# Gated recurrent mixer with its products grouped by array shape and its norm inside the loop; spatial gate with its bias added on VectorE

## The reference

```python
f = lb + (1.0 - lb) * sigmoid(fl);  k = 1.0 - f;  b = cumsum(log(f))      # within a chunk
q_dec, k_inv, k_state = q * exp(b), k * exp(-b), k * exp(b_last - b)
A = where(causal, q_dec @ k_inv.T, 0)                # 64 x 64 in each chunk
U = k_state.T @ iv                                   # 128 x 128 in each chunk
s_prev = scan(state = exp(b_last) * state + U)       # eight chunks, one after the other
o = A @ iv + q_dec @ s_prev
o = o * rsqrt(mean(o * o) + 1e-6) * onorm_g * silu(g);   return o @ w_out
```

```python
mixed = einsum('gts,bnsgc->bntgc', tril(sgu_w), v) + transpose(sgu_b)[:, :, None]
return (u * mixed) @ w_out
```

## Time and profile before

| | before |
|---|---|
| median of 3 runs (lowest to highest) | 4350.57 us (4349.04 to 4352.63) |
| the profiled execution, its own time | 4350.56 us |
| its span in the trace | 4348.7 us |
| TensorE matmuls, busy | 3777.4 us (87%) |
| VectorE, busy | 2104.5 us (48%) |
| ScalarE, busy | 1231.2 us (28%) |
| mean granted TensorE clock | 0.904 of full speed |

### The profile page before, as it was taken

The page is one execution under the profiler, slowest core; times in us unless marked ns, Lnnn a source line. Parts: engine busy times, 40 slices in busy tenths (PEclk is TensorE's granted clock), DMA queues, the critical chain, the costliest instruction groups (busy, mean ns, idle before and its releaser), DMA issues. The chain is left out here.

```text
span 4348.7 us, 57875 instructions
## 1 busy us (share of the span) xinstructions
PE 3777.4 (87%) x23603; PEld 3021.9 (69%) x23603; DVE 2104.5 (48%) x2957; ACT 1231.2 (28%) x1606; POOL 0.2 (0%) x4
## 2 busy tenths in 40 slices
PE   7899999988899988889989989979248757989998
PEld 6567887767788875568867668868147744667886
DVE  3475655343574553553443363442755546435434
ACT  2353333231342322232232132221411122223222
POOL 0000000000000000000000000000000000000000
PEclk9999999985899998889999799989569976999999
DMA  3101222210122221022222012221000010022221
GB/s 130 58 0 68 97 90 94 97 68 0 49 97 97 97 80 68 10 78 90 94 92 77 28 70 97 97 74 66 10 7 4 7 36 1 29 87 76 90 97 67
DMA packets 43411, 279.58 MB, mean 64 GB/s; under 512 B 5920, under 2 KB 6816, under 8 KB 10598
## 3 DMA queue, kind: packets, MB, share of 16 engines
q1 hardware_dynamic: 36576, 266.35, 17.3%
q10 hardware_dynamic: 6662, 10.69, 0.7%
HBM read 274.92 MB, written 2.11 MB: 64 GB/s over the span
## 5 line engine op out<-in xcount | busy, mean ns | idle before, releaser
L213 PE MATMUL PS<-XH,WH 128*128 128x512 f32 (+1 forms) x2704 | 1041.4, 385 | 27.3 <-DVEq L95 23.5
L214 PE MATMUL PS<-XL,WH 128*128 128x512 f32 (+1 forms) x2704 | 1042.7, 386 | 0.0
L215 PE MATMUL PS<-XH,WL 128*128 128x512 f32 (+1 forms) x2704 | 1037.6, 384 | 0.0
L146 DVE TENSOR_TENSOR WL<-W,WH 128x2048 fp32r<-128x2048 f32 x254 | 582.1, 2292 | 886.4 <-ACT WH L136 880.9
L136 ACT ACTIVATE WH<-W 128x2048 fp32r<-128x2048 f32 x254 | 485.6, 1912 | 1227.6 <-PE PS L303 682.3
L213 PEld LDWEIGHTS PS<-XH,WH 128*128 128x128 f32 x2704 | 510.0, 189 | 145.6 <-issue 20.2
L214 PEld LDWEIGHTS PS<-XL,WH 128*128 128x128 f32 x2704 | 509.2, 188 | 108.8 <-issue 2.2
L215 PEld LDWEIGHTS PS<-XH,WL 128*128 128x128 f32 x2704 | 510.4, 189 | 104.4
L301 PE MATMUL PS<-HH,WH 128*128 128x512 f32 (+1 forms) x1024 | 401.9, 392 | 10.5 <-DVEq L95 9.3
L302 PE MATMUL PS<-HL,WH 128*128 128x512 f32 (+1 forms) x1024 | 400.1, 391 | 0.0
L303 PE MATMUL PS<-HH,WL 128*128 128x512 f32 (+1 forms) x1024 | 399.9, 391 | 0.0
(11 more groups left out here) (435 smaller groups left out, 4217.4 us busy)
## 6 DMA issues: line engine op xcount, KB each, us to landing
W<-in_weights SPq DMA_DIRECT2D x254, 1024.0 KB, 4.8
X<-in_x ACTq DMA_DIRECT2D x1, 2048.0 KB
out<-X ACTq DMA_DIRECT2D x1, 2048.0 KB, 7.1
consts<-in_consts ACTq DMA_DIRECT2D x1, 1026.0 KB
bias<-bias_spread ACTq DMA_DIRECT2D x4, 256.0 KB
w_gd<-in_w_gd ACTq DMA_DIRECT2D x1, 640.0 KB
rope<-in_c_rope ACTq DMA_DIRECT2D x1, 528.0 KB
ws<-in_ws ACTq DMA_DIRECT2D x1, 512.0 KB
```

The costliest lines, as they stand in the source:

```text
L146: P.e.tensor_tensor(K.WL[:, s, :], K.W[:, s, :], K.WH[:, s, :].bitcast(F32), ALU.subtract).then_inc(P.sem("weights_split"), P.adds("weight ...
L213: P.e.matmul(out, wh[:, k, c], xh[:, k, r], start=(k == 0), stop=False)
L214: P.e.matmul(out, wh[:, k, c], xl[:, k, r], start=False, stop=False)
L215: last = P.e.matmul(out, wl[:, k, c], xh[:, k, r], start=False, stop=(k == KT - 1))
```

## The change

In the mixer:

- `h_i` is no longer staged; TensorE transposes `i1` directly. The loops are written out, eight steps each.
- TensorE runs the eight products with `aT` together, before it waits for the states, and then the eight with the state.
- `h_ks` is made by one multiplication of `h_ki` by exp(b) at the chunk's end. The subtraction and the third exponential go.
- The copy of `ksT` moves from VectorE to ScalarE.
- The norm moves into the loop: one product 512 columns wide with a matrix of 1/128 (`inv_dv`) gives the means on every partition; ScalarE takes (mean + eps)^(-1/2) as exp(-0.5 ln(...)) (`root`); VectorE multiplies two heads later (`normed`), and the split follows. A table set with both functions is loaded ahead. The diagonals, spreading products, reciprocal and square root after the loop go.

In the gate the bias is loaded as 128 equal rows (512 KB instead of 4 KB) and added by VectorE, which then multiplies by `u2`; the bias products go. The copy of `s_vT` moves from VectorE to ScalarE.

```diff
 # Hgrn, VectorE
-            P.e.tensor_tensor(K.h_ks[:, b, :], K.h_k[:, :], K.h_ks[:, b, :], ALU.mult)
+            P.e.tensor_tensor(K.h_ki[:, b, :], K.h_k[:, :], K.h_ki[:, b, :], ALU.mult).then_inc(P.sem("ki_ready"), P.adds("ki_ready"))
+            P.e.tensor_tensor(K.h_qd[:, b, :], K.q1h[:, t, :], K.h_eb[:, b, :], ALU.mult).then_inc(P.sem("qd_ready"), P.adds("qd_ready"))
+            P.e.wait_ge(P.sem("ki_ready"), P.due("ki_ready", 0))
+            P.e.tensor_tensor(ks, ki, ends, ALU.mult).then_inc(P.sem("keys_ready"), P.adds("keys_ready"))
...
+        def normed(t):
+            o = K.f1[:, t, :]
+            P.e.wait_ge(P.sem("o_root"), P.due("o_root"))
+            P.e.scalar_tensor_tensor(o, o, K.p["hgrn_onorm_g"][:, t:t + 1], K.o_sq[:, t % 2, :], ALU.mult, ALU.mult).then_inc(P.sem("o_normed"), P.adds("o_normed"))
+            P.e.wait_ge(P.sem("o_normed"), P.due("o_normed", 0))
+            P.e.tensor_tensor(o, o, K.g1[:, t, :], ALU.mult).then_inc(P.sem("o_gated"), P.adds("o_gated"))
...
+        keys(0)
         for t in range(8):
+            if t >= 2:
+                normed(t - 2)
             if t < 7:
-                diagonals(t + 1)
+                decays(t + 1)
+            masked(t)
+            if t >= 2:
+                low_part(t - 2)
+            states(t)
+            if t < 7:
+                keys(t + 1)
+        normed(6)
+        normed(7)
+        low_part(6)
         low_part(7)
...
 # Hgrn, ScalarE
+        P.e.preload_act_table_set("natural_log_exp_and_others")
...
+        def root(t):
+            r = K.o_sq[:, t % 2, :]
+            P.e.wait_ge(P.sem("o_mean"), P.due("o_mean"))
+            P.e.activation(r, K.PS[:, 1, :], ACT.Ln, bias=K.eps_col[:, 0:1]).then_inc(P.sem("o_logged"), P.adds("o_logged"))
+            P.e.wait_ge(P.sem("o_logged"), P.due("o_logged", 0))
+            P.e.activation(r, r, ACT.Exp, scale=-0.5).then_inc(P.sem("o_root"), P.adds("o_root"))
...
 # Hgrn, TensorE
-            for j in range(4):
-                last = P.e.matmul(K.PS[:, 1, 2 * j:2 * j + 2], K.o_sq[:, 128 * j:128 * j + 128], K.inv_dv[:, 0:2], start=True, stop=True)
+            P.e.matmul(K.PS[:, 1, :], K.inv_dv[:, :], K.o_sq[:, t % 2, :], start=True, stop=True).then_inc(P.sem("o_mean"), P.adds("o_mean"))
...
             P.e.wait_ge(P.sem("A_ready"), P.due("A_ready"))
+            for n, half, j, c in chunks:
+                P.e.matmul(K.PS[:, (7, 3)[n % 2], 64 * j:64 * j + 64], K.iT[half, j, :], K.aT[half, 64 * j:64 * j + 64],
+                           start=(j == 0), stop=False)
             P.e.wait_ge(P.sem("states_ready"), P.due("states_ready"))
             for n, half, j, c in chunks:
-                out = K.PS[:, (7, 3)[n % 2], 64 * j:64 * j + 64]
-                P.e.matmul(out, K.iT[half, j, :], K.aT[half, 64 * j:64 * j + 64], start=True, stop=False)
-                last = P.e.matmul(out, K.sp[:, n, :], K.h_qd[:, b, c], start=False, stop=True)
+                last = P.e.matmul(K.PS[:, (7, 3)[n % 2], 64 * j:64 * j + 64], K.sp[:, n, :], K.h_qd[:, b, c],
+                                  start=False, stop=(j == 3))
 # SpatialGate, VectorE and TensorE
-                P.e.tensor_tensor(K.v2[:, t - 1, :], K.PS[:, 2 + (t - 1) % 2, :], K.u2[:, t - 1, :], ALU.mult).then_inc(P.sem("sgu_gated"), P.adds("sgu_gated"))
+                P.e.tensor_tensor(v.rearrange("p (a n) -> p a n", a=4), K.PS[:, 2 + (t - 1) % 2, :].rearrange("p (a n) -> p a n", a=4), bias, ALU.add).then_inc(P.sem("sgu_biased"), P.adds("sgu_biased"))
+                P.e.wait_ge(P.sem("sgu_biased"), P.due("sgu_biased", 0))
+                P.e.tensor_tensor(v, v, K.u2[:, t - 1, :], ALU.mult).then_inc(P.sem("sgu_gated"), P.adds("sgu_gated"))
...
-                    P.e.matmul(out, K.s_vT[:, (t - 1) % 2, c], K.ws[:, t - 1, :], start=True, stop=False)
-                    last = P.e.matmul(out, K.one_row2[0:1, 0:128], K.sgu_b[0:1, t - 1, :], start=False, stop=True)
+                    last = P.e.matmul(out, K.s_vT[:, (t - 1) % 2, c], K.ws[:, t - 1, :], start=True, stop=True)
```

## The result

The changed kernel takes 4237.18 us (median of 4 runs, 4232.94 to 4240.70); the kernel before took 4349.81 us beside it (4347.70 to 4352.63). The ratio is 0.974, with a 95% interval of 0.9723 to 0.9757. The forecast was 4240, in 4226 to 4271. The profiled execution took 4240.70 us, its span is 4238.9.

The account below looks back on a forecast made before the run. Both changed stages were taken as TensorE's, slowed by changes of array shape at a low clock. Savings of 8.4 (start), 53.8 (loop), 21.0 (end) and 27.0 (gate) made 110 us: 4350.6 to 4240 us, range 4226 to 4271.

Parts of the forecast that it names:

- Start and first head: Mixer's start to the first copy-out: earlier keys and grouped products at 1.2 GHz, 8.4 us saved.
- Loop: Mixer's seven further heads: 9.3 us each instead of 16.98, 53.8 us saved.
- VectorE's 8.9 with 0.4 of waits: Mixer's loop: VectorE's summed passes of 8.9 us plus 0.4 of waits make a head of 9.3 us.
- The clock: Mixer's loop: TensorE at the higher level for most of it, a clock above 0.8.
- The first rival: Mixer stays at 1.2 GHz: TensorE bounds a head at 13.4 us, 81 us saved, 4269 us; chance 0.22.
- A change of shape: TensorE products in turns: each change of array shape costs 0.24 us at 1.2 GHz.
- Grouping gives nothing: Rival: 0.62 us is the cost of a product with its accumulation, not of shape; 4302 us, chance 0.05.
- 15 changes fewer: Mixer's head: estimate from the skill's page, 2.7 us for each head where the rows give 3.6; not used further.
- End: Mixer's last products to the next stage: 7.6 us instead of 28.6, 21.0 us saved.
- Gate: Gate's eight tiles: 2.9 us each on TensorE at 1.2 GHz instead of 6.4, 27.0 us saved.
- Costed at nothing: Table load back at the next norm (1.3 us if uncovered), the bias's 512 KB (2 to 3 us uncovered).
- Straight code fetched too slowly: Rival: the mixer's written-out heads run TensorE dry; 4360 us at 15 us more a head, chance 0.02.

Follow-up runs that it names:

- e7: The changed kernel with one more operation on VectorE in every head, a reciprocal of 128x128 values that nobody reads; 4240.16 us.
- e8: The changed kernel with TensorE turning the next head's `i` ahead of its wait for the states, and ScalarE's next exponentials ahead of `root`; 4240.21 us.
- e1: The changed kernel with the `aT` and state products in turns again, behind the wait for the states; 4296.98 us, ratio 0.988.
- e3: The changed kernel with the two kinds of product in turns, ordered so that none adds to the place just written; 4279.16 us, ratio 0.9836.
- e4: The kernel before with only the sixteen products reordered: `aT` group ahead of the wait for the states, then the state group; 4294.54 us, ratio 0.9872.
- e6: The changed kernel with the gate's bias again added by TensorE, four products grouped behind the tile's four; 4248.00 us, ratio 0.9773.
- e10: e8 with ScalarE's copies of the transposed `i` and keys ahead of the copy-out; 4266.98 us, ratio 0.9806.
- e2: The changed kernel with both product groups kept, but the `aT` group also behind the wait for the states; 4247.22 us, ratio 0.9763.
- e12: e10 with the norm's high part first in ScalarE's turn and the gates' logarithms taken head by head; 4231.67 us, ratio 0.9724.
- e9: The changed kernel with the next head's transposes and `A` ahead of the state products, keys and copies moved to match; 4231.69 us, ratio 0.9734.
- e11: The changed kernel with five 512-column products that nobody reads in TensorE's idle time at the mixer's start; 4237.69 us, ratio 0.9747.

## Why the prediction was right

By its own terms, with the working in the prediction and the measured values from the traces of before and after:

- **Start and first head**, 8.4 forecast, 28.26 - 20.56 = 7.7 measured. At 1.2 GHz throughout, as taken.
- **Loop**, 53.8 forecast, 118.88 - 65.26 = 53.6 measured: heads of 9.32 for 9.3. The number is right, and its two terms are not. "VectorE's 8.9 with 0.4 of waits" was to make the head. VectorE does set the pace where the clock is at its upper level and nothing holds it up, but with 8.2 us and not 8.9: the 8.9 was a sum of durations, and passes overlap, 0.69 long and 0.60 apart. The other 1.1 of the mean head are waits, and not 0.4 (less what the first and the last turn lack in passes): for ScalarE's exponentials behind `root`, which the prediction had named, and for TensorE's `A` and `U` in the stretches at 0.50. So VectorE is busy in 79% of the loop, where over 90% was foretold. Two errors of 0.7 us a head cancelled, and that was luck. e7 and e8 bear out the bound: one pass more costs 0.73 of a head without a pause, and heads freed of the waits stop at 8.24.
- **The clock**, taken above 0.8 for the loop: 0.86. The first rival (1.2 GHz throughout, 4269) did not come; the changed kernel's loop is at that level for its first 5.8 us and for 3 to 7 us each at 983, 1000 and 1020.
- **A change of shape**, 0.24 us at 1.2 GHz: 0.26, and 0.17 at the higher level (e1, e3). "Grouping gives nothing", which would have been 4302, is refuted by e4 alone. The prediction's "15 changes fewer" are 14, nineteen less five; its sum doesn't use them.
- **End**, 21.0 forecast, 28.57 - 7.66 = 20.9 measured; 7.66 for 7.6.
- **Gate**, 27.0 forecast, 54.92 - 22.51 = 32.4 measured; this term was mis-sized. It was worked out at 1.2 GHz, from the clock before, for TensorE's 2.9 us a tile. Once grouped it ran at 0.94, where TensorE is busy 1.65 of a tile, and VectorE's 2.60 set the pace (2.8 had been added up, again from overlapping passes). e6 shows that the bias could have stayed on TensorE, once its products were grouped.
- **Costed at nothing**: the table load did come back (5 at that line, 4 before; 1.28 us). It lies in the rest, which is 4.8 us longer than before and scatters by more than that, so neither its price nor the bias's DMA is told apart.
- **Straight code fetched too slowly**: no product of the loop waits for issue, only weight loads, 6.3 us in all, 3.1 of them with the `aT` group in the states' shadow.

The sum: 7.7 + 53.6 + 20.9 + 32.4 = 114.6, less 4.8 in the rest, is the 109.8 between the two spans. Forecast were 110. That the sum came out so close is luck too: the gate gave 5.4 more than forecast, and the rest, which moves by more than that by itself, took 4.8.

## What to carry to other kernels

Order the products of a loop by the shape that they take of the array first (it was half of the gain here), accumulations too: write all first halves, then all second halves, and the first halves can stand ahead of the wait for the second's operands. Take an engine's bound from a stretch in which it runs without a pause, start to start (8.2 us here): summed durations were too high (8.9), the loop's busy time over its seven heads too low (7.3). Then ask which waits come on top of it. When a step moves up in a queue, look at what now stands behind it: e10 lost 27 us by one step that had never been seen in a wait.

## What was not expected of the hardware

Two stretches in which TensorE is busy for nearly the same share run at different clocks. In the gate before it was busy 52.7 of 55 us at 0.50, in e6's gate, with the same products in groups, 22.11 of 24.30 at 0.92. The loop has the same, with TensorE busy for 86 to 93% in all four: e1 in turns 0.59, e3 in turns in another order 0.70, e4 grouped 0.69, the changed kernel 0.86. Grouping was paid twice in the gate. One part is the change of shape: a product with `ws` takes 0.73 us in turns (2404.29 to 2405.02) and 0.47 in a group at the same clock of 0.50 (e2, four of them from 2330.47 to 2332.34). The other is the clock that came with it; in the loop the clock came less plainly (e3 has as high a one as e4), and how much of e4's 55 us is due to it was not taken apart.

The clock also took back much of what the later orders gave. At a clock of 1.00 heads take 8.2 us in e8 and e12 and 8.8 in e9, and others, partly or wholly at 1.2 GHz, up to 12.7, 11.3 and 9.5. What decides in which head it falls stays open: e11 could raise it with idle products, not hold it.
